# Fetching and reducing the lambda vectors one pass earlier in a fused attention layer

## The reference

```python
def diff_lambda(lq1, lk1, lq2, lk2, lam_init):
    f = jnp.float32
    return (jnp.exp(jnp.sum(lq1.astype(f) * lk1.astype(f), axis=-1))
            - jnp.exp(jnp.sum(lq2.astype(f) * lk2.astype(f), axis=-1)) + lam_init)
# in diff_attention:
        p = jax.nn.softmax(s, axis=-1)
        p = p[:, :, 0] - lam[None, :, None, None] * p[:, :, 1]
```

## Time and profile before

| | |
|---|---|
| median of 3 executions | 1254.17 us (1253.95 to 1255.1) |
| profiled execution, its own time | 1255.1 us |
| its span in the profile | 1253.5 us |
| PE busy | 1222.7 us (98%) |
| DVE busy | 800.0 us (64%) |
| ACT busy | 619.1 us (49%) |
| POOL busy | 258.3 us (21%) |
| mean granted TensorE clock | 0.997 |

### The profile page before, as it was taken

How to read it: one execution, slowest core, us unless ns; L and a number is a source line. 1 busy time by engine, 2 the same in 40 slices (tenths; PEclk the granted TensorE clock), 3 DMA queues, 4 the chain that set the end, 5 groups by cost and what they waited for, 6 DMA issues and landing times.

```text
span 1253.5 us, 16906 instructions
## 1 busy us (share of the span) xinstructions
PE 1222.7 (98%) x6251; PEld 991.3 (79%) x6251; DVE 800.0 (64%) x1242; ACT 619.1 (49%) x1296; POOL 258.3 (21%) x439
## 2 busy tenths in 40 slices
PE   5899999999999999999999999999999999999996
PEld 3455778888888888888888888888888888888885
DVE  4455488667586776755546374554647675789774
ACT  5522325645555465565556555656556765312223
POOL 1211033012031040222221221222223322211111
PEclk9999999999999999999999999999999999999998
DMA  9999242222221232322222121222224423756544
GB/s 348 371 377 349 84 110 76 62 71 74 76 96 44 67 106 53 100 60 83 71 61 86 51 91 51 82 59 83 59 72 133 139 83 98 254 187 228 184 135 177
DMA packets 130482, 156.45 MB, mean 125 GB/s; under 512 B 8304, under 2 KB 97040, under 8 KB 129632
## 3 DMA queue, kind: packets, MB, share of 16 engines
q1 hardware_dynamic: 116528, 109.60, 26.7%
q0 software_dynamic: 13424, 45.20, 11.4%
q10 hardware_dynamic: 448, 0.57, 0.1%
HBM read 144.18 MB, written 11.16 MB: 124 GB/s over the span
## 4 chain that ended last, share of the span: by engine, by line
PE 92%; SPq 3%; DVE 2%; DMA 1%; ACT 1%; POOL 1%; issue 0%; POOLq 0%; DVEq 0%; ACTq 0%
PE z_ps L704 24%; PE z_ps L706 23%; PE z_ps L705 23%; PE ring L795 5%; PE ring L884 4%; SPq L658 2%; PE ring L829 2%; PE ring L828 2%; PE ring L730 2%; PE ring L888 2%; DMA ada_raw<-in_w_ada_dram 1%; PE ring L706 1%; PE ring L705 1%; PE ring L891 1%; PE ring L704 1%
## 5 line engine op out<-in xcount | busy, mean ns | idle before, releaser
L704 PE MATMUL z_ps<-w_hi,xt_hi 128*128 128x512 f32 x1350 | 554.1, 410 | 2.6 <-issue 1.1
L706 PE MATMUL z_ps<-w_hi,xt_lo 128*128 128x512 f32 x1350 | 527.7, 391 | 0.0
L705 PE MATMUL z_ps<-w_lo,xt_hi 128*128 128x512 f32 x1350 | 527.2, 391 | 0.0
L1007 ACT ACTIVATE w_hi<-w_raw 128x512 fp32r<-128x512 f32 x270 | 169.3, 628 | 334.9 <-PE z_ps L706 309.2
L704 PEld LDWEIGHTS z_ps<-w_hi,xt_hi 128*128 128x128 f32 x1350 | 254.0, 188 | 68.1 <-issue 27.2
L1441 DVE TENSOR_TENSOR w_lo<-w_raw,w_hi 128x512 fp32r<-128x512 f32 x270 | 196.8, 732 | 162.6 <-ACT w_hi L1007 162.2
L706 PEld LDWEIGHTS z_ps<-w_hi,xt_lo 128*128 128x128 f32 x1350 | 253.4, 188 | 55.3
L705 PEld LDWEIGHTS z_ps<-w_lo,xt_hi 128*128 128x128 f32 x1350 | 254.8, 189 | 38.8
L1542 DVE TENSOR_REDUCE small<-s_sb 128x2 f32<-128x1536 f32 (+1 forms) x60 | 87.6, 1460 | 20.6 <-ACT s_sb L1007 20.6
L1153 ACT ACTIVATE s_sb<-s_sb,small 128x768 f32<-128x768 f32 (+1 forms) x120 | 98.0, 821 | 3.6 <-DVE small L1542 3.5
L1902 POOL TENSOR_TENSOR sg<-sg,zs 128x128 f32<-128x128 f32 (+1 forms) x60 | 38.6, 644 | 276.2 <-DVE sg L1511 275.6
(11 more groups left out here) (196 smaller groups left out, 1378.3 us busy)
## 6 DMA issues: line engine op xcount, KB each, us to landing
w_raw<-in_w_in_dram SPq DMA_DIRECT2D x188, 256.0 KB, 3.1
ada_raw<-in_w_ada_dram SPq DMA_DIRECT2D x64, 512.0 KB, 11.6
w_raw<-in_w_out_dram SPq DMA_DIRECT2D x64, 256.0 KB, 3.8
gate_raw<-in_w_ada_dram POOLq DMA_DIRECT2D x12, 1024.0 KB, 8.0
w_raw<-in_w_in_dram POOLq DMA_DIRECT2D x20, 256.0 KB, 6.3
o_spill<-row_st POOLq DMA_DIRECT2D x14, 320.0 KB, 3.4
row_st<-o_spill POOLq DMA_DIRECT2D x14, 320.0 KB, 3.3
x_sb<-in_x_sample_dram SPq DMA_DIRECT2D x4, 1024.0 KB, 9.6
```

The lines of the kernel that those rows point to most:

```text
L704: pe.matmul(out, hi_l, hi_r, start=start, stop=False)
L705: pe.matmul(out, hi_l, lo_r, start=False, stop=False)
L706: return pe.matmul(out, lo_l, hi_r, start=False, stop=stop)
L1007: return act.activation(out, in_, ACT.Copy, **kw)
```

## The change

The transfers are issued at pass 0, step 13 instead of pass 1, step 9; products, sums, `Exp` and the last two operations are done at pass 0, step 15 (q = 23) instead of pass 1, step 14 (q = 30). Nothing is added to or taken from what is computed.

```diff
@@ ACT
-                if it == G_IT and s == KT - 2:
+                if it == KV_IT and s == KT - 1:
                     act.wait_ge(lam_ready, 1)
                     act.activation(lam[:, 2:4, :], lam[:, 0:2, :], ACT.Exp).then_inc(lam_ready, 1)
@@ POOL
-                if (it, c_step) == (G_IT, 1):
+                if (it, s) == (KV_IT, KT - 3):
                     load_lambda()
```

## The result

| | |
|---|---|
| before, median of 6 | 1254.59 us (1253.95 to 1255.48) |
| changed, median of 6 | 1258.98 us (1258.05 to 1260.21) |
| ratio, 95% interval | 1.0035 [1.0023, 1.0048] |
| profiled execution of the changed kernel | 1260.21 us, span 1258.6 us |
| mean granted TensorE clock | 0.994 |

The forecast was 1257.6 us in a range of 1256.2 to 1258.9: the direction is right, and the time lies 0.1 us above the range. The difference is 4.39 us where 3.4 was forecast (1257.6 less the 1254.17 from which it counts).

A forecast was written before the change was run, and what follows sets the result against it. PE, busy 98% of the span, was taken as the bound. A 2.65 us stall plus 0.89 us more key wait gave 3.54; 3.34 to 3.54 on the median 1254.17 gave 1257.5 to 1257.7, forecast 1257.6, range 1256.2 to 1258.9.

The forecast's parts named there:

- the price of the clock: Rival: PE's clock halves after the q = 24 stall, one step takes 6.80 instead of 3.40 us, 1261.1; within 7%.
- the case of +4.3 and more: Clock loss or another late step on top of both waits, +4.3 to +8 us; chance 7%.
- The stall at q = 24: PE waits for pass 0's first z_add: DVE's block needs 3.54 us, slack is 0.89, so it stalls 2.65 us.
- The second wait: PE's wait for the first key split, behind q = 32's weight transfer, grows from 0.90 to 1.79 us: 0.89 more.
- The moved transfers: Four issues go ahead of the root in POOL's list, landing by 145, 8 us before DVE wants them: no cost.
- the term d: Possible saving, 0 to 1.1 us, if q = 32's 4.20 us weight transfer shortens once the lambda transfers are gone.
- The old place: Removing the block before pass 1's z_add saves 0, since the bank was free 0.27 us before PE needed it.

The follow-up runs named there:

- filled and padded kernel: Changed kernel plus 16 transposes in PE's stall at q = 24 and 32 at PE's start; 1258.03 and 1258.34 us against 1253.94 and 1253.96 before.
- e4: Kernel before with only the lambda transfers moved early (pass 0, step 13), the lambda block left at pass 1, step 14; 1254.26 us against 1254.19.
- e3: Against the changed kernel, lambda block two steps earlier, at pass 0, step 13 (q = 21), transfers issued at the same point; 1254.46 us against 1254.19 before.
- unfilled kernels: Changed kernel with 48 transposes at PE's start and none in the stall, run twice; 1258.16 and 1258.58 us against 1253.94 and 1253.96 before.

## Why the prediction missed its range

The failed step is the price of the clock, which the sum put at nothing (step 3 below). That the time lies only just outside the range, and not inside it, is chance. The forecast counts from 1254.17 us, and in the result the kernel before took 1254.59: 0.42 us of the 1.4 us between 1257.6 and 1258.98 are this shift, and the measured difference of 4.39 us would lie inside the range, which spans +2.0 to +4.7 about 1254.17. That the range stops below the case of +4.3 and more, as the prediction says, is also not so; it takes in the first 0.4 us of it.

1. **The stall at q = 24: right.** Forecast 2.65 us, measured 2.77 in each of seven profiles with the whole block in this place. The extra 0.1 us lies between the end of `z_add` and PE's start: 157.53 + 0.68 = 158.21 to 158.37 is 0.16 us where 0.05 was taken from another place.
2. **The second wait: the sum right, its split not.** Forecast was that PE is dragged back by the whole block, 3.54 us from a profile with the long transfer in both kernels, or 3.34 to 3.54 against a usual execution. The filled and padded kernel, which has this mechanism and nothing else, has T = 25.11 to 25.12 against 21.57: 3.55 us. The key wait in it is 0.5 to 0.6 us instead of the 1.79 of the sum, since the transfer takes 3.2 us instead of 4.20, and in the second profile of before it is nothing instead of 0.90. In the changed kernel itself there is no key wait, because the lost clock holds PE back for longer.
3. **The clock: this step failed.** It stood among the rivals with the reason "The rows hold a longer idleness than this stall at full clock, so I hold it unlikely", within a case of 7%. It came in every profile of the changed kernel. The row at the end of the span shows the clock at 1.00 for at least 2.76 us after the last matmul, and one such stretch was taken as if it bounded all. Here 2.61 us of idleness were followed by the half clock, in another kernel 1.81 us were, and in a third 2.20 us were not: the length of the idleness alone does not decide it. Its price was also mis-sized: not a whole step (3.4 us) but 7 matmuls, 1.54 us, and of these only 0.6 to 0.8 on top of the forecast, because the key wait shrinks. With it the stretch loses 4.1 to 4.4 us (T 25.68 to 25.94 against 21.57), as much as the medians (4.16 to 4.62). But this step alone doesn't settle the miss: the filled and padded kernels keep the clock, and their medians are still 4.09 and 4.38 above before, 0.5 to 0.8 us more than their T. In their two profiles such an excess stands behind T: there they take 939.3 and 938.6 us up to the gate sums instead of the 937.5 of an execution without a wait, and ahead of T 0.9 and 0.3 us less than 154.8.
4. **The moved transfers: right.** Issued from 136.4 on, landed within 7.9 us, no cost (e4: +0.07 us). When they stay late the weight transfer can still be short (second profile of before), so the term d rested on a chance reading.
5. **The old place: right.** Removing the block there gave nothing: with block and transfers both out of the way (e3) the time is that of before.
6. **What stays open.** The wait at the gate sums (0.7 to 1.4 us at L922 or its shifted line) is in the profiles of both kernels and missing in others of both; it adds scatter. It stands in 6 of the 8 profiles with the whole block right ahead of or behind the `z_add` of pass 0, and in 3 of the 7 others, which is too few to say that the change makes it more frequent. That the lost clock lengthens the whole time is argued from T alone: the medians of filled and unfilled kernels do not resolve it. And the 0.5 to 0.8 us by which the filled ones exceed their T have the size of the wait at the gate sums and stand at its place in their profiles, but whether it is in their usual execution is not shown.

## What to carry to other kernels

Moving work earlier is free only into idle time of its own engine. Ahead of an instruction that empties the banks of the busiest engine it costs its whole length less the slack there, here 0.8 to 0.9 us, and where a second chain on the same engine also bounds the busy one further down, as that to the keys does here, the slack is lost again there. When such a move leaves the matmul engine idle for some 2 us or more (here the clock was lost after 1.81 and 2.61 us, and kept after 2.20 once), count with the loss of the clock: price it by the matmuls that start behind the stall, and look for the next wait, which takes part of it back. One profile is one draw: a wait of 0.9 us behind a transfer should be seen twice before it enters a sum.

## What the runs showed that was not expected

TensorE's clock fell after 2.61 us of idleness in the middle of the kernel, in 4 profiles of 4 with the empty stall, though it held for at least 2.76 us at the end of another and for 2.20 us before the keys in a third, and 16 transposes inside the stall kept it in 3 of 3. And a fetch of 16 KB of instructions takes time on the same 16 DMA engines as the data, by the profile's count (5.5% of them in 2 us). Where it began within 2.2 us of the issue of a weight transfer, in three profiles, the transfer took 4.5 to 5.0 us instead of 3.2. The kernel before with 12 transposes added at the start of its program was 2.65 us slower, of which the longer transfer accounts for about 1.3.
